# Weights stored by the host in the order of their loads, one contiguous run per partition

## The reference

```python
u = _rmsnorm(h, norm1_w[l])
proj = u @ w_in[l]                                    # (B,T,D_IN)
aq, ak, av, gq, gk, gv, g_lr, g_r, gate_a, gate_b = jnp.split(proj, offs, axis=-1)
attn_o = _swa_sink_attention(aq, ak, av, attn_sinks[l])
gate_logit = (g_lr @ gla_gate_w2[l] + gla_gate_b[l]).astype(jnp.float32)
log_a = jax.nn.log_sigmoid(gate_logit) / GLA_GATE_NORMALIZER
gla_o = _gla(gq, gk, gv, log_a)
gla_o = _rmsnorm(gla_o, gla_norm_w[l]) * jax.nn.silu(g_r)
merged = jax.nn.sigmoid(gate_a) * attn_o + jax.nn.sigmoid(gate_b) * gla_o
h = h + merged @ w_out[l]
v2 = _rmsnorm(h, norm2_w[l])
ff = jax.nn.silu(v2 @ w_ffn_gate[l]) * (v2 @ w_ffn_up[l])
h = h + ff @ w_ffn_down[l]
return _rmsnorm(h, final_norm_w)
```

## Time and profile before

| | |
|---|---|
| median of 3 runs | 3782.68 us (3782.21 to 3783.95) |
| profiled execution | 3786.89 us |
| span of its slowest core (core 5) | 3785.3 us |
| spans of all cores | 3775.6 to 3785.3 us |
| PE busy | 3695.9 us, 98% |
| DVE, ACT, POOL busy | 32%, 25%, 20% |
| POOL's DMA queue (q0) | 373,856 packets, 268.58 MB, 53.3% |
| SP's DMA queue (q1) | 52,320 packets, 97.06 MB, 9.6% |

### The profile page before, as it was taken

The page is one execution under the profiler, slowest core; times in us unless marked ns, Lnnn a source line. Parts: engine busy times, 40 slices in busy tenths (PEclk is TensorE's granted clock), DMA queues, the critical chain, the costliest instruction groups (busy, mean ns, idle before and its releaser), DMA issues.

```text
span 3785.3 us, 50247 instructions; the slowest of 8 cores (3775.6 to 3785.3 us)
## 1 busy us (share of the span) xinstructions
PE 3695.9 (98%) x18688; PEld 1717.2 (45%) x18688; DVE 1200.2 (32%) x1919; ACT 964.9 (25%) x2028; POOL 755.6 (20%) x756
## 2 busy tenths in 40 slices
PE   5999999999999999999999999999999999999998
PEld 3444444444444444444444444444444444444443
DVE  4677534422311011111127774434223111100003
ACT  2455433423200000011125544433241000000000
POOL 2233333432100000000003323334311010100000
PEclk8999999999999999999999999999999999999999
DMA  9535375449965656378683443565399777763566
GB/s 135 79 49 70 39 95 79 55 74 169 162 90 75 81 68 88 61 125 151 118 122 55 61 65 48 81 95 84 53 212 142 112 124 129 108 81 65 117 118 161
DMA packets 426416, 368.84 MB, mean 97 GB/s; under 512 B 13728, under 2 KB 378272, under 8 KB 426048
## 3 DMA queue, kind: packets, MB, share of 16 engines
q0 software_dynamic: 373856, 268.58, 53.3%
q1 hardware_dynamic: 52320, 97.06, 9.6%
HBM read 586.78 MB, written 47.38 MB: 168 GB/s over the span
## 4 chain that ended last, share of the span: by engine, by line
PE 90%; DMA 4%; DVE 3%; issue 2%; ACT 1%; POOL 0%; SPq 0%; DVEq 0%; ACTq 0%; POOLq 0%
PE ps L368 79%; PE psS L368 8%; DMA hd<-hw 2%; DMA xn<-x 1%; PE ps L705 1%; PE psS L506 1%; ACT a_P L373 0%; DVE gl L766 0%; DMA out<-hsl 0%; DVE a_sel L667 0%; ACT gl L373 0%; DVE gm L376 0%; DVE a_sm L670 0%; DVE a_sd L688 0%; ACT L373 0%
## 5 line engine op out<-in xcount | busy, mean ns | idle before, releaser
L368 PE MATMUL ps<-X,wsl 128*128 128x512 bf16 x8832 | 1943.2, 380 | 2.6 <-DVE X L376 2.6
L368 PEld LDWEIGHTS ps<-X,wsl 128*128 128x128 bf16 x8832 | 853.5, 98 | 1044.5 <-issue 45.0
L368 PE MATMUL ps<-wsl,X 128*128 128x512 bf16 (+1 forms) x3328 | 723.8, 373 | 0.6 <-DMA wsl<-w_in 0.6
L368 PEld LDWEIGHTS ps<-wsl,X 128*128 128x128 bf16 x3328 | 323.3, 98 | 350.5 <-issue 1.6
L376 DVE TENSOR_TENSOR ffT<-ps,silu 128x512 bf16<-128x512 f32 x176 | 121.7, 692 | 1051.3 <-PE ps L368 1051.3
L373 ACT ACTIVATE silu<-ps 128x512 bf16<-128x512 f32 x176 | 105.1, 597 | 1101.8 <-PE ps L368 1101.8
L368 PE MATMUL ps<-wsl,ffT 128*128 128x512 bf16 x1716 | 379.2, 379 | 1.0 <-DVE ffT L376 1.0
L368 PEld LDWEIGHTS ps<-wsl,ffT 128*128 128x128 bf16 x1716 | 167.0, 98 | 199.0 <-issue 1.5
L368 PE MATMUL psS<-wsl,ffT 128*128 128x512 bf16 x1100 | 244.8, 379 | 0.0
L349 POOL DMA_DIRECT2D wsl<-w_g x44 | 51.3, 1165 | 954.7 <-PE ps L368 954.4
L368 PE MATMUL ps<-wsl,mT 128*128 128x512 bf16 x1024 | 227.0, 381 | 2.1 <-DVE hw L376 2.1
(11 more groups left out here) (164 smaller groups left out, 2506.9 us busy)
## 6 DMA issues: line engine op xcount, KB each, us to landing
wsl<-w_in POOLq DMA_DIRECT2D x40, 2048.0 KB, 19.5
wsl<-w_g POOLq DMA_DIRECT2D x44, 1024.0 KB, 11.6
wsl<-w_u POOLq DMA_DIRECT2D x44, 1024.0 KB, 15.8
wsl<-w_d POOLq DMA_DIRECT2D x16, 1920.0 KB, 15.4
hsl<-hd SPq DMA_DIRECT2D x96, 256.0 KB, 6.6
wsl<-w_in POOLq DMA_DIRECT2D x20, 1024.0 KB, 15.3
hw<-x SPq DMA_DIRECT2D x64, 256.0 KB, 10.3
wsl<-w_out POOLq DMA_DIRECT2D x8, 2048.0 KB, 27.4
```

The lines of the kernel that those rows point to most:

```text
L368: ins = e.matmul(o_, lhsT=l_, rhs=r_, start=s0, stop=s1)
```

## The change

The host writes each weight matrix in the order of the loads (`_pack`): part after part, and within a part, partition after partition, all blocks of that partition behind each other. A load of a part then is one contiguous run per partition (`blk`). The 16 gate columns are stored beside the 256 value columns and come with them in one part of 272 columns. Since the parts of a slot now lie one behind the other, matmuls read them through `wview`; and those of the GLA queries and keys and of gate and up wait for their own part alone (`wkeys`). The other lines of the diff pass the view in place of the slot's number.

```diff
+
+
+def in_groups():
+
+    out = [[[(O_AV, 256), (O_GLR, 16)]], [[(O_AK, 256)]]]
+    for kvh in range(4):
+        out += [[[(O_AQ + kvh * 512, 512)]], [[(O_GA + kvh * 512, 512)]]]
+    for h in range(4):
+        out.append([[(O_GQ + h * 256, 256)], [(O_GK + h * 256, 256)]])
+        out += [[[(o + h * 512, 512)]] for o in (O_GV, O_GR, O_GB)]
+    return out
+
+
+IN_BLOCKS = [[sum(n for _, n in part) for part in b] for b in in_groups()]
...
         for p, (dst_fn, src) in enumerate(parts):
-            S.op("pool", (lambda e, dst_fn=dst_fn, src=src, slot=slot: e.dma_start(out=dst_fn(wsl[slot].ap), in_=src)),
+            S.op("pool", (lambda e, dst_fn=dst_fn, src=src, slot=slot: e.dma_start(out=dst_fn(wsl[slot].flat), in_=src)),
                  writes=wkeys(slot, p, len(parts)), dma=True, chan=("w", slot, p))
...
-    def full(w_, src, c0, n=512):
-        return [((lambda d, n=n: d[:, :, 0:n]), src[:, :, c0:c0 + n])]
+    def wview(slot, k, n, part=0):
+        return wsl[slot].flat[:, part * k * n:(part + 1) * k * n].rearrange("p (k c) -> p k c", k=k)
+
+    def blk(src, e0, n, d0=0):
+
+        return ((lambda d: d[:, d0:d0 + n]), src[e0:e0 + 128 * n].rearrange("(p c) -> p c", p=128))
...
-        wlist.append([((lambda d: d[:, :, 0:256]), w_in_v[:, :, O_AV:O_AV + 256]),
-                      ((lambda d: d[:, :, 256:272]), w_in_v[:, :, O_GLR:O_GLR + 16])])
-        wlist.append(full(0, w_in_v, O_AK, 256))
-        for kvh in range(4):
-            wlist.append(full(0, w_in_v, O_AQ + kvh * 512))
-            wlist.append(full(0, w_in_v, O_GA + kvh * 512))
-        for h in range(4):
-            wlist.append([((lambda d: d[:, :, 0:256]), w_in_v[:, :, O_GQ + h * 256:O_GQ + (h + 1) * 256]),
-                          ((lambda d: d[:, :, 256:512]), w_in_v[:, :, O_GK + h * 256:O_GK + (h + 1) * 256])])
-            wlist.append(full(0, w_in_v, O_GV + h * 512))
-            wlist.append(full(0, w_in_v, O_GR + h * 512))
-            wlist.append(full(0, w_in_v, O_GB + h * 512))
+        e0 = 0
+        for cols in IN_BLOCKS:
+            parts, d0 = [], 0
+            for n in cols:
+                parts.append(blk(w_in, e0, KC * n, d0))
+                d0 += KC * n
+                e0 += 128 * KC * n
+            wlist.append(parts)
         for g in range(4):
-            wlist.append(full(0, w_out_v, g * 512))
+            wlist.append([blk(w_out, g * D * 512, KC * 512)])
         for j in range(HC // 2):
-            wlist.append([((lambda d: d[:, :, 0:256]), w_g_v[:, :, j * 256:(j + 1) * 256]),
-                          ((lambda d: d[:, :, 256:512]), w_u_v[:, :, j * 256:(j + 1) * 256])])
+            wlist.append([blk(w_g, j * D * 256, KC * 256), blk(w_u, j * D * 256, KC * 256, KC * 256)])
+        e0 = 0
         for g in range(4):
-            k0 = 0
             for np_ in PIECES:
-                wlist.append([((lambda d, np_=np_: d[:, 0:np_, :]), w_d_v[:, k0:k0 + np_, g * 512:(g + 1) * 512])])
-                k0 += np_
+                wlist.append([blk(w_d, e0, np_ * 512)])
+                e0 += 128 * np_ * 512
...
-    def grp_feat(slot, c0, m, tb, evac):
+    def grp_feat(w, wk, c0, m, tb, evac):
         b = bank("m")
-        mm([(ps[b][0:m, :], wsl[slot].ap[:, k, c0:c0 + m], X.ap[:, k, tb * 512:(tb + 1) * 512], k == 0, k == KC - 1)
-            for k in range(KC)], wres(slot) + XTB[tb], [("ps", b)])
+        mm([(ps[b][0:m, :], w[:, k, c0:c0 + m], X.ap[:, k, tb * 512:(tb + 1) * 512], k == 0, k == KC - 1)
+            for k in range(KC)], wk + XTB[tb], [("ps", b)])
         evac(b)
 
-    def grp_tok(slot, c0, n, t, evac):
+    def grp_tok(slot, n, t, evac):
         b = bank("m")
-        mm([(ps[b][:, 0:n], X.ap[:, k, t * 128:(t + 1) * 128], wsl[slot].ap[:, k, c0:c0 + n], k == 0, k == KC - 1)
...
-                grp_feat(slot, dk * 128, 128, tb, evq)
+                grp_feat(wview(slot, KC, 256), wkeys(slot, 0, 2), dk * 128, 128, tb, evq)
...
-                grp_feat(slot, 256 + dk * 128, 128, tb, evk)
+                grp_feat(wview(slot, KC, 256, 1), wkeys(slot, 1, 2), dk * 128, 128, tb, evk)
...
             bg = bank("m")
-            mm([(ps[bg][:, :], wsl[slot].ap[:, k, sub * 128:(sub + 1) * 128],
+            wg, wu = wview(slot, KC, 256), wview(slot, KC, 256, 1)
+            mm([(ps[bg][:, :], wg[:, k, sub * 128:(sub + 1) * 128],
                  X.ap[:, k, tb * 512:(tb + 1) * 512], k == 0, k == KC - 1) for k in range(KC)],
-               wres(slot) + XTB[tb], [("ps", bg)])
+               wkeys(slot, 0, 2) + XTB[tb], [("ps", bg)])
             sl = silu[n[0] % 3]
             n[0] += 1
...
-            mm([(ps[bu][:, :], wsl[slot].ap[:, k, 256 + sub * 128:256 + (sub + 1) * 128],
+            mm([(ps[bu][:, :], wu[:, k, sub * 128:(sub + 1) * 128],
                  X.ap[:, k, tb * 512:(tb + 1) * 512], k == 0, k == KC - 1) for k in range(KC)],
-               wres(slot) + XTB[tb], [("ps", bu)])
+               wkeys(slot, 1, 2) + XTB[tb], [("ps", bu)])
...
+def _pack(w, blocks):
+
+    out = np.empty(w.size, np.float32)
+    e0 = 0
+    for k0, nk, runs in blocks:
+        rows = w[k0 * 128:(k0 + nk) * 128].reshape(nk, 128, -1)
+        b = np.concatenate([rows[:, :, c:c + n] for c, n in runs], axis=2).transpose(1, 0, 2)
+        out[e0:e0 + b.size] = b.reshape(-1)
+        e0 += b.size
+    assert e0 == w.size
+    return out
+
+
...
+        "w_in": _pack(f(inputs["w_in"])[0], [(0, KC, part) for b in in_groups() for part in b]),
```

More of the change, by code:

```diff
@@ L197, in build_nc @@
     x = din("x", [T, D])
[L198 to L202, removed]
+    w_in = din("w_in", [D * DIN])
+    w_out = din("w_out", [D * D])
+    w_g = din("w_g", [D * FF])
+    w_u = din("w_u", [D * FF])
+    w_d = din("w_d", [FF * D])
     n1 = din("n1", [128, KC])
@@ L215, in build_nc @@
     sd = nc.dram_tensor("sd", [4, 128, 1024], F32, kind="Internal").ap()
[L217 to L221, removed]
     TOTAL = 212736
@@ L528, in norm1_tile @@
         yield
-    def grp_feat(slot, c0, m, tb, evac):
+    def grp_feat(w, wk, c0, m, tb, evac):
         b = bank("m")
-        mm([(ps[b][0:m, :], wsl[slot].ap[:, k, c0:c0 + m], X.ap[:, k, tb * 512:(tb + 1) * 512], k == 0, k == KC - 1)
-            for k in range(KC)], wres(slot) + XTB[tb], [("ps", b)])
+        mm([(ps[b][0:m, :], w[:, k, c0:c0 + m], X.ap[:, k, tb * 512:(tb + 1) * 512], k == 0, k == KC - 1)
+            for k in range(KC)], wk + XTB[tb], [("ps", b)])
         evac(b)
-    def grp_tok(slot, c0, n, t, evac):
+    def grp_tok(slot, n, t, evac):
         b = bank("m")
-        mm([(ps[b][:, 0:n], X.ap[:, k, t * 128:(t + 1) * 128], wsl[slot].ap[:, k, c0:c0 + n], k == 0, k == KC - 1)
+        w = wview(slot, KC, n)
+        mm([(ps[b][:, 0:n], X.ap[:, k, t * 128:(t + 1) * 128], w[:, k, :], k == 0, k == KC - 1)
             for k in range(KC)], wres(slot) + xk(t), [("ps", b)])
@@ L588, in evv @@
                 par.append(glr_tr(t))
-            grp_tok(vslot, 0, 272, t, evv)
+            grp_tok(vslot, 272, t, evv)
             tick()
@@ L598, in evk @@
                              ps[b][a * 64:a * 64 + 64, :], [("ps", b)], kT[kk].f(tb * 512, (tb + 1) * 512))
-            grp_feat(slot, kp * 128, 128, tb, evk)
+            grp_feat(wview(slot, KC, 256), wres(slot), kp * 128, 128, tb, evk)
             tick()
@@ L608, in evq @@
                 copy("act", aq.ap[:, pr, :], ps[b][:, :], [("ps", b)], aq.k(pr, pr + 1))
-            grp_feat(slots[0], pr * 128, 128, tb, evq)
+            grp_feat(wsl[slots[0]].ap, wres(slots[0]), pr * 128, 128, tb, evq)
             if pr == 3 and tb == 1:
@@ L617, in evg @@
                 ts("pool", asg.ap[:, pr, :], tmp.ap, 0.5, 0.5, ALU.mult, ALU.add, tmp.all, asg.k(pr, pr + 1))
-            grp_feat(slots[1], pr * 128, 128, tb, evg)
+            grp_feat(wsl[slots[1]].ap, wres(slots[1]), pr * 128, 128, tb, evg)
             if pr == 3 and tb == 1:
@@ L929, in evv @@
                     copy("act", g_v[t % 4].ap, ps[b][:, :], [("ps", b)], g_v[t % 4].all)
-                grp_tok(sv, 0, 512, t, evv)
+                grp_tok(sv, 512, t, evv)
                 if t == NTL - 1:
@@ L941, in evr @@
                     stt(rs.ap, tmp.ap, 1.0, ps[b][:, :], ALU.add, ALU.mult, tmp.all + [("ps", b)], rs.all)
-                grp_tok(sr, 0, 512, t, evr)
+                grp_tok(sr, 512, t, evr)
                 if t == NTL - 1:
@@ L952, in evb @@
                     tt("pool", rs.ap, rs.ap, gnws.ap, ALU.mult, rs.all + gnws.all, rs.all)
-                grp_tok(sb2, 0, 512, t, evb)
+                grp_tok(sb2, 512, t, evb)
                 if t == NTL - 1:
@@ L1309, in make_in_maps @@
     shared = {
[L1310 to L1314, removed]
+        "w_in": _pack(f(inputs["w_in"])[0], [(0, KC, part) for b in in_groups() for part in b]),
+        "w_out": _pack(f(inputs["w_out"])[0], [(0, KC, [(g * 512, 512)]) for g in range(4)]),
+        "w_g": _pack(f(inputs["w_ffn_gate"])[0], [(0, KC, [(j * 256, 256)]) for j in range(HC // 2)]),
```

(3 more changed lines are left out.)

## The result

The changed kernel takes 3831.73 us (median of 4 runs) beside 3783.11 before; the ratio is 1.0119, 95% interval 1.0105 to 1.0133. I had forecast 3772. One of the four runs (4424.69 us) and some runs of most experiments had cores at a lower granted clock for whole stretches; the ratios leave out those that this made clearly longer, and where smaller cases remain, as in the last two ratios, the interval is wide. The profiled execution took 3830.32 us; its slowest core is core 3.

What follows compares the result with a forecast made beforehand. TensorE, busy 98% of 3785.3 us, was taken as the bound. The profiled 3786.89 less 5.8 (start) and 6.3 (output projection) gives 3774.8; from the runs' median 3770.6 or 3774.8; in the middle 3772, range 3764 to 3782 us.

Steps and rivals of the forecast that it cites:

- What is late next: SP's transfers: SP transfers beside weight loads: pieces four times as long make them 9 us or more, no more than 10.6 now.
- The output projection: Late cores 5 and 1 come down to core 6 as weights need less DMA time: 6.3 us won, 0 to 7.6.
- The start: Token tile 4 lands earlier behind faster loads of slots 0 and 1: 5.8 us won, bounds 4.2 and 8.5.
- The second half's start: The chain through a store of `hsl`, 8.42 us beside weight loads, stays: between 3 us better and 3 us worse.
- Halves waited for singly and POOL's fewer loads: Matmuls waiting for their own part, and two fewer load issues on POOL: worth nothing while loads land in time.
- Rival C: Slower: SP starves behind long pieces in the output projection, 11 us late in each half; 3802 us, chance 0.10.
- D: Slower: long runs starting 32 KB apart read badly, at the start and in the output projection; 3800 us, chance 0.04.
- A's sign: Tile 4 after 40 us would show that bytes alone count and the output projection stays: 3781 us, chance 0.16.
- B's: A core with 124 us again would show the start gains, the output projection does not: 3777 us, chance 0.12.

Runs made afterwards that it cites:

- piece1: The changed kernel with every weight load in pieces of one block (1024 bytes, 512 in half slots), laid one after another in HBM; ratio to before 1.0008.
- same_layout: The changed kernel with its order in HBM, blocks permuted within each run, but each load split so that no piece exceeds one block; ratio to before 0.9981.
- start_long: The changed kernel with one run per partition only for the program's first four loads, pieces of one block in all others; ratio to before 0.9981.

## Why the prediction was wrong

**The step that failed** is "What is late next: SP's transfers", where I set an SP transfer at "9 us or more", "no more than now (10.6 us)". For the median that held (7.9 after, 9.3 before). But PE is stopped by the latest transfer, not by the median one, and the lead of four tiles is 14 us. Transfers issued while two weight loads begin took 16 to 23 us. I had scaled from one small load behind pieces of 4096 bytes, which gave a bound from below, and took the bound for the value: alone, with no other transfer of SP, it is 17.9 us beside 16 KB pieces. The price of a queue, several SP transfers behind each other, I had put at nothing; how much it adds is not shown. That the weight loads are over sooner, which I counted as relief, is true as well (20.5 us to landing for `w_u` in the second output projection instead of 47.1), but it doesn't help the latest transfer.

**The output projection**, minus 6.3, had the wrong sign for this reason: it lost 6.4 and 19.9 us. That the weights need less DMA time there was right and is not what bounds the stage.

**The start**, minus 5.8, had the mechanism right in part and was too large. On core 3 ACT begins on tile 4 at 39.05 us, 3.3 earlier than on core 5 of before, not at 36.6, and PE's gap shrinks from 9.98 to 7.40:

```profile
39.05 1.91 ACT L527 ACTIVATE X<-xn 128x2048 bf16<-128x2048 bf16 x1 [6.46 <-DMA xn<-x]
...
43.64 1.01 PE L513 MATMUL psS<-identb,xn 128*128 128x128 bf16 x8 [7.40 <-DVE gst L406]
```

The rates that I took from the earlier trace rows for pieces of 1024 and 4096 bytes, 153 and 167 GB/s, are 9% apart, but they come from different stretches with different company; alone, loads in pieces of 4 and 1 KB are 2.8% apart (77.4 and 79.6 us). The rule of the Trainium skill, "DMA: Bandwidth & Descriptors", section Specifications, that 512 B is enough for line-rate, put the gain at 0.7 us; the 3.3 lie halfway, and no run here timed 512-byte pieces alone. Nor is all of it the length. On the mean of the eight cores tile 4 starts at 43.0 us before, at 38.6 after, and already at 41.6 with pieces of one block (`piece1`) and at 40.7 in `same_layout`: 1.3 to 2.3 of the 4.4 us come with short pieces. In both, the gate columns' own load is gone, for which I had 0.7, and the order in HBM is new; no run separates these two.

**The second half's start**, between 3 better and 3 worse, was 7.7 us worse: 13.2 us of `gst` instead of 5.5, the same failed step. The down stage, where `hsl` is loaded, I had put at nothing without a reason; PE waits 6.4 us there, for the same cause. The lower clock behind such stalls was in no term of the sum.

**Halves waited for singly and POOL's fewer loads** at nothing: right as far as the run with pieces of one block can tell (1.0008, 0.9996 to 1.0021).

**Rival C**, to which I gave 0.10, is what happened, in the place it names: SP's transfers fall behind long pieces in the output projection. It priced that at 11 us in each half, 22 in all, and measured are 6.4 and 19.9, 26.3 in all; that the sums are near is in part luck. It put 3 us on the second half's start, where 7.7 were lost, and nothing on the down stage and the clock, so that its 3802 is 30 us short. What I held against it, six tiles loaded ahead, is true only of the first tiles of the stage. D fell with `same_layout` and, for the long runs themselves, with the weights alone. A's sign, tile 4 after 40 us, did not come; B's, a core with 124 us, was passed by every core (125.8 us or more), by C's mechanism.

What stays open: why an output projection spares some cores and not others (it is late on cores 1 and 5 of before in the first half, on cores 4 and 5 of `start_long` in the second). The cores are out of step there by a few us; whether that decides was not tried.

## What to carry to other kernels

A longer piece made its own transfer a little cheaper here and the other queue on the same DMA engines later; look for the transfers with a deadline, and compare the worst landing, not the median, with the lead that the code gives them. Where a run of pieces must be long, give the others more lead, more than the worst landing on any core, or use it only where nobody else waits, as at this kernel's start. A stage that runs at PE's pace before a DMA change can be one late tile from not doing so.

## What the runs showed that I had not expected

Between pieces of 1 and 16 KB the weight loads alone differ by 4% (79.6 and 76.6 us for six loads of 2 MB on each of 8 cores), while a 256 KB load on SP's queue beside them goes from 8.2 to 17.9 us, and nearly all of that lies between 4 and 16 KB. POOL's issue becomes cheaper with fewer pieces: 1178 ns for 16 pieces per partition, 563 for one.
